# DeepNorm layer with PEER: product shapes and evacuation of the last 24 groups of U

## The reference, cut to what matters

```python
s = einsum(q, subkeys); sv, si = top_k(s, 16)          # per head, two halves of 128 keys
eidx = the 16 best of 16 x 16 pairs; gates = softmax(best)
act = gelu(einsum('td,thkd->thk', x, u_tab[eidx]))      # 16384 experts, d = 1024
y = einsum('thk,thkd->td', gates * act, v_tab[eidx])
```

## Time and profile before

| | |
|---|---|
| median of 3 runs | 1024.97 us (1024.19 to 1026.61) |
| the profiled execution | 1025.29 us |
| its span, first to last instruction | 1023.5 us |
| mean granted TensorE clock | 0.992 of full speed |
| PE / DVE / ACT / POOL busy | 98% / 76% / 50% / 31% |

### The profile page before, as it was taken

One profiled execution on the slowest core, in us unless ns is written; L12 is line 12 of the kernel. 1 busy time (PEld: TensorE's weight loads), 2 busy tenths in 40 slices (PEclk: granted clock), 3 DMA queues, 4 the chain that ended last, 5 costly groups with the idle time before them and its releaser, 6 DMA issues.

```text
span 1023.5 us, 17998 instructions
## 1 busy us (share of the span) xinstructions
PE 1004.8 (98%) x6863; PEld 929.8 (91%) x6863; DVE 778.7 (76%) x1592; ACT 514.4 (50%) x756; POOL 322.0 (31%) x206
## 2 busy tenths in 40 slices
PE   7999999999999999999999999999999999999996
PEld 7999889989999999999999999988888888888785
DVE  7978888874899698886687788766666867776666
ACT  5785656545444544445444434454554545545443
POOL 2001000011887478777778777000010000000002
PEclk9999999998999999999999999999999999999998
DMA  9879868676555587778766666667779788887761
GB/s 356 354 284 373 288 193 298 250 228 207 169 181 171 160 207 185 186 175 193 168 149 144 149 161 146 180 212 220 217 231 328 225 248 262 265 274 216 222 189 44
DMA packets 96854, 222.80 MB, mean 218 GB/s; under 512 B 27520, under 2 KB 45952, under 8 KB 96000
## 3 DMA queue, kind: packets, MB, share of 16 engines
q1 hardware_dynamic: 74336, 207.93, 62.7%
q0 software_dynamic: 22144, 13.71, 8.9%
q10 hardware_dynamic: 288, 0.01, 0.0%
HBM read 211.06 MB, written 10.55 MB: 217 GB/s over the span
## 4 chain that ended last, share of the span: by engine, by line
PE 93%; DVE 3%; DMA 1%; ACT 1%; POOL 0%; issue 0%; POOLq 0%; ACTq 0%; DVEq 0%
PE px L1161 33%; PE pw L862 17%; PE pw L863 17%; PE pw L864 17%; PE px L1137 3%; DMA ada<-in_ada 1%; PE px L1106 1%; PE pv L862 1%; PE pv L864 1%; PE pv L863 1%; DVE w_lo L1215 0%; DVE part L1264 0%; PE px L862 0%; PE px L863 0%; PE px L864 0%
## 5 line engine op out<-in xcount | busy, mean ns | idle before, releaser
L567 ACT ACTIVATE w_hi<-raw 128x1024 fp32r<-128x1024 f32 x312 | 328.7, 1057 | 317.8 <-PE px L1161 159.9
L1215 DVE TENSOR_TENSOR w_lo<-raw,w_hi 128x1024 fp32r<-128x1024 f32 x285 | 347.3, 1225 | 135.4 <-ACT w_hi L567 133.2
L862 PE MATMUL pw<-a_hi,w_hi 128*128 128x256 f32 x1280 | 368.1, 288 | 0.6 <-DVE a_lo L1482 0.6
L864 PE MATMUL pw<-a_hi,w_lo 128*128 128x256 f32 x1280 | 363.3, 284 | 0.0
L863 PE MATMUL pw<-a_lo,w_hi 128*128 128x256 f32 x1280 | 363.3, 284 | 0.0
L540 POOL DMA_INDIRECT gates_spill<-gate,place x128 | 227.4, 1777 | 83.9 <-issue 46.3
L862 PEld LDWEIGHTS pw<-a_hi,w_hi 128*128 128x128 f32 x1280 | 246.7, 193 | 2.2 <-issue 1.2
L863 PEld LDWEIGHTS pw<-a_lo,w_hi 128*128 128x128 f32 x1280 | 246.9, 193 | 0.1
L864 PEld LDWEIGHTS pw<-a_hi,w_lo 128*128 128x128 f32 x1280 | 246.6, 193 | 0.0
L1161 PE MATMUL px<-w_hi,ws_hi 128*128 128x512 f32 x512 | 158.8, 390 | 0.0
L1161 PE MATMUL px<-w_lo,ws_hi 128*128 128x512 f32 x512 | 158.5, 389 | 0.0
(11 more groups left out here) (348 smaller groups left out, 1154.3 us busy)
## 6 DMA issues: line engine op xcount, KB each, us to landing
raw<-in_u SPq DMA_DIRECT2D x128, 512.0 KB, 4.3
raw<-in_v SPq DMA_DIRECT2D x128, 512.0 KB, 4.8
raw<-in_ws SPq DMA_DIRECT2D x56, 512.0 KB, 5.9
ada<-in_w_ada SPq DMA_DIRECT2D x32, 512.0 KB, 6.9
gates_spill<-zero POOLq DMA_DIRECT2D x16, 512.0 KB, 7.0
g_row<-gates_spill SPq DMA_DIRECT2D x128, 64.0 KB, 4.6
ada<-in_ada SPq DMA_DIRECT2D x6, 1024.0 KB, 10.5
raw<-in_w SPq DMA_DIRECT2D x7, 768.0 KB, 10.6
```

The lines of the kernel that those rows point to most:

```text
L567: return nc.scalar.activation(out, in_, ACT.Copy, **kw)
L862: nc.tensor.matmul(out, lh, rh, start=start and x == 0, stop=False)
L864: last = nc.tensor.matmul(out, ll, rh, start=False, stop=stop and x == len(pairs) - 1)
L1215: v.tensor_tensor(w_lo[:, m % RING], raw[:, m % RING], w_hi[:, m % RING].bitcast(F32), ALU.subtract).then_inc(lo_ready, 1)
```

## The change

From group 40 (`WIDE = 40`, the 41st) on, 24 groups or 48 pieces:

- **PE**: the two parts of the activations lie side by side in `a_both`. For each chunk the high part of the weights meets both in one matmul of 512 columns, and the low part meets the high part in one of 256: 16 matmuls a piece in place of 24. A piece fills a whole bank: pw[g%2] for its group's first piece, pv[g%2] for the second. Columns 0 to 255 hold two of the three products, columns 256 to 511 the third.
- **ACT**: works by pieces. Iteration p waits for piece p, copies columns 256 to 511 to `u_sum` (SBUF), applies gelu to piece p-1 out of `u_sum`, then `split_hi(p+4)` and, if p has a one-hot step, `take_upper`.
- **DVE**: iteration p begins with `add_halves(p-1)` (bank columns 0 to 255 plus `u_sum`), then, at an odd p, `gate_u(p//2 - 1)`, now two instructions, one for each bank; then the rest as before. gelu of piece p-1 waits for its add.

The waits of PE on `u_out` and `u_gated` are unchanged. The new one on `idx_ready` is for bank pv[1].

```diff
--- before.py
+++ after.py
...
 OH = P // 4
 OH_AT = [82 + 11 * n // 8 for n in range(OH)]
 GA_U = OH_AT[0] // 2
+WIDE = 40
 ZERO = 256
 ZERO_DMAS = 16
 
...
         raw = sb("raw", 0, [RING, 1024])
         w_hi = sb("w_hi", 4096, [RING, 1024], F32R)
         w_lo = sb("w_lo", 8192, [RING, 1024], F32R)
-        a_hi = sb("a_hi", 12288, [KC, T], F32R)
-        a_lo = sb("a_lo", 14336, [KC, T], F32R)
+        a_both = sb("a_both", 12288, [2, KC, T], F32R)
+        a_hi, a_lo = a_both[:, 0], a_both[:, 1]
         SM, AR = 16384, 17344
         small_at = [SM]
 
...
         ws_lo = sb("ws_lo", AR + 33792, [RING, T], F32R)
         idx = sb("idx", AR + 34816, [3, P])
         g_row = sb("g_row", AR + 34816, [RING, P])
+        u_sum = sb("u_sum", R0 + 2560, [2, T])
+        assert base + 4 * (R0 + 3072) <= nc.sbuf_usable_end
         assert base + 4 * (R0 + 2944) <= nc.sbuf_usable_end
 
 
...
 
             bank = pv[0] if t == 1 and k in (2, 3) else px[2 * t + k // 4]
             return bank[:, (k % 4) * P:(k % 4 + 1) * P]
+
+        def u_bank(g, e):
+
+            return (pw, pv)[e][g % 2]
 
         def acc_bank(b):
 
...
         idxT_done, idx_ready = sem("idxT_done"), sem("idx_ready")
         scattered = sem("scattered")
         g_landed = [sem(f"g_landed{s}") for s in range(RING)]
+        u_half_copied, u_summed = sem("u_half_copied"), sem("u_summed")
+        u_first_out = sem("u_first_out")
         u_out, u_gated, w_gated = sem("u_out"), sem("u_gated"), sem("w_gated")
         oh_ready, oh_used, g_lower_taken, g_upper_taken = (sem(s) for s in (
             "oh_ready", "oh_used", "g_lower_taken", "g_upper_taken"))
...
                 copy(W[:, row:NK, t:t + 4], px[n % 4][:, :].rearrange("p (t j) -> p j t", t=4)[:, row:NK]) \
                     .then_inc(g_upper_taken, 1)
 
+            def gelu(p):
+
+                g, e = divmod(p, 2)
+                act.wait_ge(u_summed, p - 2 * WIDE + 1)
+                left = T - 4 * taken(g)
+                last = nc.scalar.activation(W[:, p, 0:left], u_sum[:, e, 0:left], ACT.Gelu)
+                if left < T:
+                    last = nc.scalar.activation(u_bank(g, e)[:, left:T], u_sum[:, e, left:T], ACT.Gelu)
+                last.then_inc(u_out if e else u_first_out, 1)
+
             for g in range(NG):
                 if g == 8:
                     act.wait_ge(x1_spilled, 16)
...
                     act.wait_ge(scattered, 16 * PH * TOPK)
                     for r in range(RING):
                         split_w(r)
+                if g >= WIDE:
+                    for e in range(2):
+                        p = 2 * g + e
+                        act.wait_ge(piece_used, UP + p + 1)
+                        if g > WIDE:
+                            act.wait_ge(u_out if e else u_first_out, g if e else g - WIDE)
+                        copy(u_sum[:, e], u_bank(g, e)[:, T:2 * T]).then_inc(u_half_copied, 1)
+                        if p > 2 * WIDE:
+                            gelu(p - 1)
+                        split_hi(UP + p + 4)
+                        if p in OH_AT:
+                            take_upper(OH_AT.index(p))
+                    continue
                 split_hi(UP + 2 * g + 4)
                 if g == INDEX_AFTER + 1:
                     act.wait_ge(idxT_done, 1)
                     copy(idx[:, :, :], pv[1][:, 0:3 * P].rearrange("p (a t) -> p a t", a=3)).then_inc(idx_ready, 1)
-                if 2 * g in OH_AT:
-                    take_upper(OH_AT.index(2 * g))
                 act.wait_ge(piece_used, UP + 2 * g + 2)
                 src = pw[g % 2][:, :].rearrange("p (j t) -> p j t", j=2)
-                left = T - 4 * taken(g)
-                last = nc.scalar.activation(W[:, 2 * g:2 * g + 2, 0:left], src[:, :, 0:left], ACT.Gelu)
-                if left < T:
-                    last = nc.scalar.activation(src[:, :, left:T], src[:, :, left:T], ACT.Gelu)
-                last.then_inc(u_out, 1)
+                nc.scalar.activation(W[:, 2 * g:2 * g + 2, :], src, ACT.Gelu).then_inc(u_out, 1)
                 split_hi(UP + 2 * g + 5)
-                if 2 * g + 1 in OH_AT:
-                    take_upper(OH_AT.index(2 * g + 1))
                 for t in range(TT):
                     if g == EXP_AFTER[t]:
                         act.wait_ge(best_ready, t + 1)
                         nc.scalar.activation(gate[t][:, :], gate[t][:, :], ACT.Exp).then_inc(gate_exp, 1)
 
+            gelu(2 * NG - 1)
             for v in range(NK - RING):
                 split_hi(VP + v + RING)
                 split_w(v + RING)
...
                         pe.wait_ge(u_out, g - 1)
                     else:
                         pe.wait_ge(u_gated, g - 1 - GA_U)
-                columns_piece(m, pw[g % 2][:, e * T:(e + 1) * T])
+                if g < WIDE:
+                    columns_piece(m, pw[g % 2][:, e * T:(e + 1) * T])
+                    return
+                if g == WIDE + 1 and e == 0:
+                    pe.wait_ge(idx_ready, 1)
+                bank = u_bank(g, e)
+                hi, lo = (w.rearrange("p (k c) -> p k c", k=KC) for w in weights(m))
+                for k in range(KC):
+                    nc.tensor.matmul(bank[:, :].rearrange("p (a t) -> p a t", a=2), hi[:, k], a_both[:, :, k],
+                                     start=k == 0, stop=False)
+                    last = nc.tensor.matmul(bank[:, 0:T], lo[:, k], a_hi[:, k], start=False, stop=k == KC - 1)
+                last.then_inc(piece_used, 1)
 
             def transposed():
 
...
 
                 dve.wait_ge(u_out, g + 1)
                 dve.wait_ge(g_upper_taken, taken(g))
-                w = W[:, 2 * g:2 * g + 2, T - 4 * taken(g):T]
-                v.tensor_tensor(w, pw[g % 2][:, :].rearrange("p (j t) -> p j t", j=2)[:, :, T - 4 * taken(g):T], w, ALU.mult) \
-                    .then_inc(u_gated, 1)
+                q = slice(T - 4 * taken(g), T)
+                for e in range(2):
+                    w = W[:, 2 * g + e, q]
+                    last = v.tensor_tensor(w, u_bank(g, e)[:, q], w, ALU.mult)
+                last.then_inc(u_gated, 1)
+
+            def add_halves(p):
+
+                dve.wait_ge(u_half_copied, p - 2 * WIDE + 1)
+                u = u_sum[:, p % 2]
+                v.tensor_tensor(u, u_bank(p // 2, p % 2)[:, 0:T], u, ALU.add).then_inc(u_summed, 1)
 
             dve.wait_ge(zero_landed, 16 * ZERO_DMAS)
             for i in range(PH):
...
                 if p == 2 * NG - 1:
                     for r in range(RING):
                         split_w(r)
+                if p > 2 * WIDE:
+                    add_halves(p - 1)
+                if p % 2 and p // 2 - 1 >= GA_U:
+                    gate_u(p // 2 - 1)
                 split_lo(UP + p + 3)
                 if p == NORMAL_AT:
                     normal(1)
...
                 if p == 2 * NG - 3:
                     for r in range(RING):
                         gate_w(r)
-                if p % 2 and p // 2 >= GA_U:
-                    gate_u(p // 2)
+            add_halves(2 * NG - 1)
             split_lo(VP + 3)
+            gate_u(NG - 1)
             gate_w(RING)
             for r in range(RING, NK):
                 if r + 1 < NK:
```

## The result

The changed kernel takes **1040.54 us** (median of four, 1039.25 to 1041.16) against 1024.9: 15.6 us slower, ratio 1.015 with a 95% interval of 1.0137 to 1.0163. The prediction said 1035.3, 1027 to 1043, slower with 83%. Direction and mechanism hold; the loss is half as large again as forecast.

A forecast was written before the change was run, and what follows sets the result against it. PE was taken to bound the kernel: 1025.29 us, less 5.05 for the wide product, plus 15.4 for 14 waits of PE, gives 1035.6, or 1035.3 as median, 10 us slower; range 1027 to 1043.

The forecast's parts named there:

- The bound: Whole kernel: PE, busy 98% of the span, sets the time; in U, time taken from PE comes off the end.
- PE's gain: Products of the 48 changed pieces in U: 0.105 us saved per piece, -5.05 us in all, range 0 to 10.
- the new piece is 8 x (226.7 + 120): PE's time per changed piece: eight 512-column products at 226.7 ns and eight of 256 at 120 ns, 2.773 us.
- The wait that follows: PE before even pieces waits for the gate of group g-2: 14 waits, +15.4 us.
- The chain from E: From PE's end of piece p's products (E) through ACT and DVE: bank free for PE at E + 4.95.
- lateness behind several steps in a row: Pieces whose previous piece also has a one-hot step: add, ACT and all behind come 0.5 us later.
- Throughput isn't the limit yet; order is: DVE in late U: load becomes some 135 of 145 us, so instruction order, not total work, makes PE wait.
- Rival 1: PE before pieces 86 to 122: chain from E under 3.66 us, no waits, only the gain left, 1019.9 us; chance 13%.
- Rival 2: All 48 pieces: the 512-column product saves nothing; 1040.4 us, less 1.5 as slower pieces cover more; chance 8%.
- Rival 3: PE's five longest waits each drop the granted clock to 1.2 GHz for a while; 1043.3 us; chance 6%.
- five long waits: PE's waits on the gate before pieces 86, 90, 104, 108 and 112, forecast at about 1.9 us each.
- What I cost at nothing: Late weight parts, even pieces without a step, and the last piece before V: no added time; weight load has some 8 us.

The follow-up runs named there:

- e6: e1 with ACT's split_hi moved ahead of gelu of the previous piece; 1020.63 us, ratio 0.9963; measured again 1022.22 us.
- e8: e6 with the 512-column product undone into two products of 256; 1025.47 us, ratio 1.0007.
- e1: Changed kernel with gate_u moved one iteration forward in DVE's list, between take_lower and the next one-hots; 1029.89 us, ratio 1.0044.
- e4: Changed kernel with DVE's first comparison of each one-hot step done twice; 1068.05 us, ratio 1.0421.
- e5: Changed kernel with ACT's split_hi moved ahead of gelu, the late gate kept; 1034.19 us, ratio 1.0095.
- e2: Changed kernel with the 512-column product undone into two products of 256, the late gate kept; 1040.66 us, ratio 1.016.
- e1n: e1 with the 512-column product undone into two products of 256; 1029.15 us, ratio 1.0043.

## Why the prediction was right or wrong

- **The bound, and the rule that any wait of PE is added to the end**: right. V starts 15.7 us later and the spans differ by 15.9.
- **PE's gain**: right sign, but too large; it was a quarter to a third less than forecast: 3.4 us by the changed kernel's trace, 3.9 by those of e6 and e8, not 5.05. The term that was off is "the new piece is 8 x (226.7 + 120)". In the changed kernel a 512 is followed by a 256 after 230 to 240 ns, not 227, and the 256 by the next 512 after about 117, not 120: pieces 80 to 82 take 2.84, 2.82 and 2.83 us (494.32, 497.16, 499.98, 502.81), not 2.773. A step and a piece take the forecast 3.66 in some places, 3.71 in others. The interval given, 0 to 10, held it. By the Trainium skill's 2.5 ns a matmul ("TensorE: Matmul & The Clock Gate", "Back-to-back issue gap") it would be 1.0; the trace agrees with neither figure and gives 3.4/384 = 9 ns, or 10 by e6 and e8.
- **The wait that follows**: right in place, kind and nearly in number, 13 for 14. It was under-sized: 17.2 us, not 15.4. The chain from E was right: behind a lone step PE restarts at E + 4.95 to 5.1, where 4.95 was forecast. What was too small is the lateness behind several steps in a row, taken as 0.5: there `take_lower` begins at E + 2.6 to 2.8 where 2.5 was forecast, and PE restarts at 5.6 to 5.75 where it was 5.45 to 5.55, in the eight waits of that kind. It was added as a fixed amount and is a loop of its own (e1, e4, e5). DVE's four comparisons play next to no part: from start to start they take 1.06 us on average, 1.03 before.
- **"Throughput isn't the limit yet; order is"**: shown by e6, which does all the work of the change with one wait of PE, and that one on a load.
- **Rival 1, the loop is covered**: false for the changed kernel, though its figure, 1019.9, is nearly what e6 takes once both orders are mended.
- **Rival 2, the wide product brings nothing**: by the time of the changed kernel it looks true (e2 takes the same), but by another mechanism than the one given: the product is faster, PE waits longer.
- **Rival 3, the clock**: given 6%, and it happened, twice in the trace rather than at all five long waits, for 3.4 us. The reason against it, "PE runs at least 5.5 us between two waits", was no protection. This, with the smaller gain (1.6) and the longer waits (1.8), is the difference between 10 and 15.6, less 1.4 of chance ahead of the stage, the clock again.
- **What I cost at nothing**: right. No wait fell on the weights' low part in the changed kernel, none on the transition to V. In e6, where PE no longer waits for the gate's order, the load that was given "some 8" us does come too late for ACT once, for V's first piece.

## What to carry to other kernels

When an evacuation gets a second engine's step, write down every loop that the hand-offs close, engines in lists and all, and compare the time round each with what PE needs per piece: the loop through PE (here its banks) is the one that shows first, but one between ACT and DVE alone may stand behind it. Inside a loop put the steps others wait for first; here two moves of lines, the gate ahead of the next one-hots and `split_hi` ahead of gelu, turned 15.6 us lost into 2.4 to 4 us gained. A gain on PE can be judged only where PE has no waits: e1 against e1n shows nothing, e6 against e8 3 to 4 us. And a step in a queue passes its own waits on to what stands behind it: `split_hi` stands ahead of `take_upper`, so a load that lands late holds up the gate.

## What the runs showed of the hardware that I had not expected

- The granted clock fell to 1.2 GHz behind waits of PE of only 1.85 and 1.9 us, with PE otherwise busy, and not behind others of the same length or longer (2.16 before piece 86; 1.91 and less in e2). Each of these two falls lasted some 3.4 us. How long PE waits doesn't alone decide it: e4 has waits of over 3 us with no fall.
- A matmul of 512 columns with its moving operand in two blocks, ahead of one of 256, took 230 to 240 ns to the next start, against 227 among its like in V. Which of the two causes the difference wasn't tried.
